# A weight queue that waits for two tiles of expert rows before the second layer, and the same queue without that wait

## The reference

```python
for l in range(DEPTH):
    h = modulate(rmsnorm(x, g_mix[l]), mod[:, 0, None], mod[:, 1, None])
    hc = modulate(rmsnorm(xc, g_mix[l]), modc[0], modc[1])
    ... = split(h @ w_in[l]); ... = split(hc @ w_in[l])
    x = x + mod[:, 2, None] * (concatenate([o_a, o_b, o_c]) @ w_out[l])
    ...
    y = grouped_moe(tokens, router_w, router_bias, w1[l], w3[l], w2[l])
    x = x + mod[:, 5, None] * y[:B * S].reshape(B, S, D)
    if not last:
        xc = xc + modc[5] * y[B * S:].reshape(B, C, D)
return rmsnorm(x, g_final)
```

## Time and profile before

| | us |
|---|---|
| median of 3 runs | 1246.97 |
| lowest and highest | 1245.11 and 1253.57 |
| the profiled execution | 1245.2 |
| its span, first to last instruction | 1243.3 |
| PE busy | 980.4 (79%) |
| DVE busy | 474.3 (38%) |
| ACT busy | 257.0 (21%) |
| POOL busy | 229.3 (18%) |
| DMA, mean over the span | 256 GB/s, 317.93 MB |

### The profile page before, as it was taken

One profiled execution on the slowest core, in us unless ns is written; L12 is line 12 of the kernel. 1 busy time (PEld: TensorE's weight loads), 2 busy tenths in 40 slices (PEclk: granted clock), 3 DMA queues, 4 the chain that ended last, 5 costly groups with the idle time before them and its releaser, 6 DMA issues. The chain is left out here.

```text
span 1243.3 us, 23462 instructions
## 1 busy us (share of the span) xinstructions
PE 980.4 (79%) x8536; PEld 530.7 (43%) x8537; DVE 474.3 (38%) x1020; ACT 257.0 (21%) x497; POOL 229.3 (18%) x380
## 2 busy tenths in 40 slices
PE   3899998998887499999889059998887387755870
PEld 1344443445445255555545044544554254322440
DVE  1267525454545423333323167317533422211223
ACT  2101121333311022222222030124321022111210
POOL 2100001120020133333333230000000123211232
PEclk9999999999977599999989679998877599877995
DMA  9987513991005649999997293311003799999973
GB/s 366 389 329 262 211 68 110 396 389 63 1 3 207 252 192 394 418 372 418 421 422 310 101 389 126 135 67 68 1 1 133 318 392 400 401 424 422 412 325 121
DMA packets 52940, 317.93 MB, mean 256 GB/s; under 512 B 7176, under 2 KB 7256, under 8 KB 30352
## 3 DMA queue, kind: packets, MB, share of 16 engines
q1 hardware_dynamic: 40144, 284.70, 56.8%
q0 software_dynamic: 9536, 20.55, 4.7%
q10 hardware_dynamic: 3200, 11.86, 2.5%
HBM read 309.13 MB, written 13.17 MB: 259 GB/s over the span
## 5 line engine op out<-in xcount | busy, mean ns | idle before, releaser
L1591 PE MATMUL ps<-ring,HT 128*128 128x512 f32 (+1 forms) x672 | 305.9, 608 | 4.1 <-issue 2.1
L1591 PE MATMUL ps<-ring,area 128*32 128x256 f32 x3936 | 244.8, 400 | 46.1 <-DMA ring<-in_w 34.8
L1591 PE MATMUL ps<-area 128*32 128x256 f32 (+5 forms) x1896 | 225.9, 391 | 27.5 <-DVE area L1499 13.9
L1591 PEld LDWEIGHTS ps<-ring,HT 128*128 128x128 f32 x672 | 129.8, 199 | 156.1 <-issue 153.0
L1591 PEld LDWEIGHTS ps<-ring,area 128*32 128x32 f32 x3936 | 131.1, 115 | 132.0 <-issue 45.4
L1591 PEld LDWEIGHTS ps<-area 128*32 128x32 f32 (+2 forms) x1896 | 122.2, 136 | 53.1 <-issue 16.0
L1517 DVE COPY area<-ps 128x256 f32<-128x256 f32 x65 | 27.6, 425 | 243.9 <-PE ps L1831 240.1
L1591 PE MATMUL ps<-HT,area 128*32 128x256 f32 x704 | 87.0, 403 | 24.5 <-DMA area<-in_w 21.2
L1048 ACT ACTIVATE area<-ps 64x256 f32<-64x256 f32 x63 | 23.8, 377 | 378.8 <-PE ps L1591 378.8
L1048 ACT ACT_TABLE_LOAD x63 | 80.8, 1283 | 44.6 <-DVEq L1510 43.5
L815 POOL DMA_INDIRECT area<-h_rows,area x68 | 71.1, 1046 | 58.1 <-POOL area L813 40.3
(11 more groups left out here) (186 smaller groups left out, 822.4 us busy)
## 6 DMA issues: line engine op xcount, KB each, us to landing
ring<-in_w SPq DMA_DIRECT2D x66, 2048.0 KB
ring<-in_w_ada SPq DMA_DIRECT2D x24, 2048.0 KB
ring<-in_w_in SPq DMA_DIRECT2D x10, 2048.0 KB
HT<-in_w SPq DMA_DIRECT2D x10, 2048.0 KB
area<-in_w SPq DMA_DIRECT2D x10, 2048.0 KB
area<-in_w SPq DMA_DIRECT2D x20, 1024.0 KB
ring<-in_w_out SPq DMA_DIRECT2D x4, 2048.0 KB
area<-expert_rows ACTq DMA_DIRECT2D x12, 512.0 KB, 6.6
```

The lines of the kernel that those rows point to most:

```text
L1591: return t_.matmul(out, lhsT, rhs, start=first, stop=last_)
```

## The change

In SP's stream, behind the gate rows, the wait on `y_in[1]` and the condition around it are taken out. Nothing else differs:

```diff
                 for cnd in range(routed(l) // S_LAT):
                     sp.dma_start(gate[:, cnd], modD[l, cnd:cnd + 1, 5 * D:6 * D].broadcast_to([P, D])).then_inc(gate2_in, 16)
-                if l < DEPTH - 1:
-
-                    sp.wait_ge(y_in[1], 32 * (l + 1))
```

## The result

Over 20 runs each, the changed kernel takes 1255.68 us in the median and the kernel before 1243.41; the ratio is 1.0091, 95% interval 1.0070 to 1.0112, so 9 to 14 us slower. (The median of three runs shown ahead of the prediction, 1246.97, lay high among the 20.) My forecast was 1248.0, in a range up to 1254.0. The kernel is slower, as forecast, but by some 12 us, where my sum had 2.0. (The forecast stood on the three runs: from the median of 20 the same 2.0 us give 1245.4, so the miss is 10 us and not 8.)

A forecast was written before the change was run, and what follows sets the result against it. Bound: a chain of POOL's last scatter and drain, y loads, DVE's adds, PE's transposes and barrier. Delay 0.5 + 0.75 x (2.5 - 0.5) = 2.0 us gave 1247.2 or 1249.0; middle taken, 1248.0; range 1243.5 to 1254.0.

The forecast's parts named there:

- No gain from earlier weights: Second layer's in-projection: its weight units were in time already, so issuing them earlier gains 0.
- Which units go, and when the stream ends: SP's queue: six units (12.6 MB) move ahead from about 666 at 387 GB/s, ending near 709.5 instead of 757.
- The y rows are late by the backlog's share: Expert-row loads after the first layer's experts: 2.5 us of weights still queued delay tile 0 by 1.25 to 2.5 us.
- So a scatter may land 0 to 3.6 us later. I take 0.5, near the lower end, because all of them together carry those 0.21 MB: POOL's last scatters of expert rows, running beside the weights: landing 0.5 us later, delaying the barrier.
- Rival B: Last four scatters, each waiting for the one before last: landing 3.6 us later costs 6.4 us, 1251.6 to 1253.4; chance 0.08.
- Rival C: Slots not free, units start only at 688, tile 0 of y rows 8.9 to 13.5 us late: 1254.1 to 1258.7; chance 0.04.
- A: No change: units run at 415 GB/s, end near 707.3, delay 0 to 0.5 us; chance 0.27 together with E.
- E: Void wait: SP's queue can't pass because a slot is held, 1245.2 to 1247; chance 0.27 together with A.
- D: Gain: PE or DVE runs the in-projection 1 to 3 us faster with memory quiet, 1242.5 to 1246; chance 0.06.
- Within 1%: Whole kernel: measured time within 1% (12.5 us) of no change, chance 0.94.
- a first add over 4 us late: DVE's first add over the y rows, forecast at 713 instead of 711.4; over 4 us late would show the forecast wrong.

## Why the prediction was wrong

- *No gain from earlier weights*: right. PE started `uc` at 749.99, 1.19 us after the barrier, and no unit was waited for, as in the earlier trace rows.
- *Which units go, and when the stream ends*: right. Six units, from 668, at some 390 GB/s, until about 712.5 (709.5 and the 2.4 us of the later issue); the second out unit at 764.5 (693.95 + 70.57), after `uc`'s product.
- *The y rows are late by the backlog's share*: the mechanism exists (2.8 us for tile 0 when the units are issued with them, 0.8 without the drain), but it cost 0.3 here, not 1.5. The scatters' delay had used up the backlog, and the constant 6.9 us of the drain came on top. My own sum said that a later barrier lets the backlog shrink; it stopped at 0.5 us.
- *"So a scatter may land 0 to 3.6 us later. I take 0.5, near the lower end, because all of them together carry those 0.21 MB"*: **this is the step that failed.** The landing went from 1.2 to 4.2 us for the last scatter, +3.0, and those before it to 4.3 to 5.4, though the last three carry next to no bytes (576 each): what a scatter sends doesn't set when its packets get their turn. The 11.5 us against 2.6 of the earlier trace rows hinted at it, and I had used them only for the y rows. And "Here the trace has no landing time" was true of the issues only: the packets of the scatter at 668.46 showed the 3.2 us (above).
- *The chain.* Rival B had the right mechanism, its condition was met (a landing over 0.8 us later), and its bound for one landing (3.6) is near the 3.0 to 4.0 measured. It was priced at 6.4 us; measured are 9.0. B counted one wait in the middle; there are two long ones (2.69 and 2.87) and a short one (0.46), because the second of the last four waits for the last scatter of the loop, which is slowed too. I gave it 0.08.
- *Rival C* had the price (8.9 to 13.5) by luck, in the wrong place: no unit started late, and the y rows didn't queue behind one. *A, E and D* are out.
- *Within 1%*: the ratio of 1.0091 just holds it, though its interval reaches 1.0112. My own sign of being wrong, a first add over 4 us late, came true: it was 9.3.

Why the packets of a scatter start 2.8 us later beside the stream (3.4 us against 0.6) isn't settled. It is not the length of the stream's rows (3.1 to 3.4 us with the long ones), and it shrinks with a shorter, slower stream (0.6 to 1.3 and 0.9 to 1.1). A stream at full rate with little under way wasn't made.

## What to carry to other kernels

A wait that holds a queue back can protect transfers that it doesn't name: before it is removed, list every transfer that will then run beside the stream, and ask of each not how many bytes it moves but how often somebody waits for its landing, one after another. Here the chain of small transfers paid the longer landing about three times (9.0 us), the same four overlapping once (3.5). A queue's packets in a window behind the issue show a landing that the issue's row doesn't give. And where all engines and the DMA are idle, look at what the profile puts there: leaving out the drain of 6.9 us at the barrier was worth more than anything tried here with the queue, though the next drain then took as long, beside other work.

## What the runs showed of the hardware

- A small indirect transfer of POOL landed 1.1 to 1.7 us after its instruction on idle engines and 4.1 to 5.4 us after it beside a stream at 390 GB/s; its first packet moved 0.6 and 3.1 to 3.5 us after it. The Trainium skill gives a memory latency that rises from 0.2 to 2 us at high load (DMA: Bandwidth & Descriptors, "Latency and other measured facts"); the rise of 3.0 us and more here is larger than that, and 2.8 us of it lie ahead of the first packet.
- POOL's drain behind the last indirect scatters took 6922 ns in every profile of the first layer's end where it was kept, with the DMA engines idle or loaded before it, though all scatters had landed. Without it the time fell by 10.5 us over the two layers, and POOL's next drain took 7540 ns instead of 669.
